# Attention with scaled probabilities turned by plain transposes and neighbourhood outputs written backwards, on one Trainium2 core

## What is computed

```python
s = jnp.einsum('bqhd,bkhd->bhqk', qblk, k).astype(jnp.float32) * scale
p = jax.nn.softmax(s, axis=-1).astype(v.dtype)
return jnp.einsum('bhqk,bkhd->bqhd', p, v)
```

## Time and profile before

| what | value |
|---|---|
| median of 3 runs | 1291.67 us |
| profiled execution | 1291.43 us |
| its span | 1289.6 us |
| mean granted PE clock | 0.934 of 2.4 GHz |
| busy share of the span | PE 88%, PEld 44%, DVE 28%, ACT 22%, POOL 8% |
| DMA | 311.67 MB, 242 GB/s mean |

### The profile page before, as it was taken

How to read it: one execution, slowest core, us unless ns; L and a number is a source line. 1 busy time by engine, 2 the same in 40 slices (tenths; PEclk the granted TensorE clock), 3 DMA queues, 4 the chain that set the end, 5 groups by cost and what they waited for, 6 DMA issues and landing times. The chain is left out here.

```text
span 1289.6 us, 19112 instructions
## 1 busy us (share of the span) xinstructions
PE 1138.2 (88%) x8093; PEld 567.9 (44%) x8093; DVE 366.6 (28%) x884; ACT 277.4 (22%) x673; POOL 103.6 (8%) x111
## 2 busy tenths in 40 slices
PE   4998999984999999999489989999579999999935
PEld 2455466542344444443144545665234444444313
DVE  3102554116122222212140056431512212222214
ACT  1111444113011111111131035430401111111112
POOL 3200000300001101100000010000010101100000
PEclk8999999986999999999679999999779999999975
DMA  9803555343499999998651155531646999999721
GB/s 363 313 16 131 215 196 197 133 175 145 150 368 371 373 373 386 379 376 317 257 188 41 66 197 214 196 131 66 245 151 231 381 366 374 382 387 384 276 107 50
DMA packets 68707, 311.67 MB, mean 242 GB/s; under 512 B 8837, under 2 KB 11105, under 8 KB 46081
## 3 DMA queue, kind: packets, MB, share of 16 engines
q1 hardware_dynamic: 58400, 288.58, 58.6%
q0 software_dynamic: 9344, 18.55, 4.4%
q10 hardware_dynamic: 864, 3.15, 0.6%
HBM read 304.24 MB, written 18.58 MB: 250 GB/s over the span
## 5 line engine op out<-in xcount | busy, mean ns | idle before, releaser
L710 PE MATMUL psum<-arena 128*64 128x512 f32 x512 | 239.0, 611 | 6.3 <-issue 4.9
L713 PE MATMUL psum<-arena 128*64 128x512 f32 x512 | 239.1, 611 | 0.0
L710 PEld LDWEIGHTS psum<-arena 128*64 128x64 f32 x512 | 68.7, 140 | 150.1 <-issue 148.1
L758 PE MATMUL psum<-arena 128*64 128x512 f32 x512 | 126.7, 616 | 2.7 <-ACT arena L1104 2.7
L1428 DVE SCALAR_TENSOR_TENSOR arena<-arena,psum 64x768 f32<-64x768 f32 x32 | 30.3, 948 | 331.2 <-ACT arena L1099 331.2
L721 PE MATMUL psum<-arena 128*32 128x256 f32 x2048 | 117.4, 381 | 0.1
L1099 ACT ACTIVATE arena<-psum 64x768 f32<-64x768 f32 x32 | 25.7, 804 | 314.1 <-PE psum L713 314.1
L721 PEld LDWEIGHTS psum<-arena 128*32 128x32 f32 x2048 | 63.4, 110 | 65.1 <-issue 27.3
L846 PE MATMUL psum<-arena 128*128 128x384 f32 x256 | 83.5, 487 | 1.2 <-PE psum L834 0.6
L987 PE MATMUL psum<-arena 128*128 128x384 f32 x256 | 83.6, 487 | 0.6 <-PE psum L987 0.6
L525 POOL DMA_INDIRECT arena<-token_rows,row_i x32 | 31.0, 970 | 519.4 <-PE psum L693 266.5
(11 more groups left out here) (223 smaller groups left out, 1224.8 us busy)
## 6 DMA issues: line engine op xcount, KB each, us to landing
arena<-in_w_gate SPq DMA_DIRECT2D x64, 1024.0 KB, 10.5
arena<-in_w_up SPq DMA_DIRECT2D x64, 1024.0 KB, 14.9
arena<-in_w_down SPq DMA_DIRECT2D x64, 1024.0 KB, 7.8
arena<-in_w_ada SPq DMA_DIRECT2D x24, 2048.0 KB, 7.8
arena<-in_w_in SPq DMA_DIRECT2D x6, 2048.0 KB, 22.1
arena<-in_w_out SPq DMA_DIRECT2D x4, 2048.0 KB, 7.7
arena<-expert_rows SPq DMA_DIRECT2D x12, 512.0 KB, 8.3
arena<-in_w_in SPq DMA_DIRECT2D x2, 1664.0 KB, 13.1
```

The costliest lines, as they stand in the source:

```text
L710: ins = nc.tensor.matmul(bank[b][0:MAIN, :], hg[:, k, 0:MAIN], wg[half][:, k % 4, :], start=(k == 0), stop=(k == KD - 1))
L713: ins = nc.tensor.matmul(bank[b][MAIN:P, :], hg[:, k, 0:MAIN], wu[half][:, k % 4, :], start=(k == 0), stop=(k == KD - 1))
L758: ins = nc.tensor.matmul(bank[6][MAIN * j:MAIN * j + MAIN, :], hidT[:, c, 0:MAIN], w[half][:, c % 2, 512 * j:512 * j + 512], start=(c == 0 ...
```

## The change

The exponentials are no longer divided by their sums on the way through PE. DVE takes one reciprocal per head as soon as that head's exponentials are there, GpSimd multiplies the head's `prob` (128 by n, in place, in SBUF) by it, and PE turns each block with a plain transpose against the identity, waiting for one head at a time. `exp_ready` is raised once per head. The reversed order of the neighbourhood queries stays in `probT` and in the product with the values; ACT undoes it by writing those outputs backwards. The diagonals and their buffer go. `unit` is moved so that GpSimd's program can use it.

```diff
@@ GpSimd, after the output DMAs of layer l have landed @@
                 pool.sem_inc(out_free, 1)
+                for u in range(UNITS):
+                    n, c = unit(u)[3], 2 * (u % 2)
+                    for i in range(2):
+                        pool.wait_ge(rsum_ready, 2 * (UNITS * l + u) + i + 1)
+                        p = prob[:, u % 2, i, 0:n]
+                        pool.tensor_scalar(p, p, rsum[:, c + i:c + i + 1], None, ALU.mult).then_inc(scaled, 1)
                 if l + 1 < DEPTH:
                     caches(l + 1)
@@ PE, scores @@
-                        pe.wait_ge(exp_ready, UNITS * l + u - 1)
+                        pe.wait_ge(exp_ready, 2 * (UNITS * l + u - 1))
@@ PE, turned @@
-                    pe.wait_ge(diag_ready, UNITS * l + u + 1)
                     for i in range(2):
+                        pe.wait_ge(scaled, 2 * (UNITS * l + u) + i + 1)
                         if u >= 1:
                             pe.wait_ge(probT_act if i == 0 else probT_dve, UNITS * l + u)
                         for c in range(n // P):
-                            ins = nc.tensor.matmul(bank[4 + i][:, P * c:P * c + P], prob[:, u % 2, i, P * c:P * c + P], diag[:, u % 2, i, :],
-                                                   start=True, stop=True)
+                            ins = nc.tensor.transpose(bank[4 + i][:, P * c:P * c + P], prob[:, u % 2, i, P * c:P * c + P], ident)
@@ ACT, exps and outputs @@
-                        ins = nc.scalar.activation(prob[:, u % 2, i, 0:n], bank[c][:, 0:n], ACT.Exp,
-                                                   bias=neg_max[:, c:c + 1],
-                                                   accum_out=sums[:, 2 * (u % 4) + i:2 * (u % 4) + i + 1])
-                    ins.then_inc(exp_ready, 1)
+                        nc.scalar.activation(prob[:, u % 2, i, 0:n], bank[c][:, 0:n], ACT.Exp,
+                                             bias=neg_max[:, c:c + 1],
+                                             accum_out=sums[:, 2 * (u % 4) + i:2 * (u % 4) + i + 1]).then_inc(exp_ready, 1)
...
-                    nc.scalar.activation(hT[:, 4 * kind + pair, P * t:P * t + P], bank[6][:, 0:P], ACT.Copy).then_inc(o_ready, 1)
+                    o = hT[:, 4 * kind + pair, P * t:P * t + P]
+                    if kind == 0:
+                        o = bass.AP(o.tensor, o.offset + P - 1, [list(o.ap[0]), [-1, P]])
+                    nc.scalar.activation(o, bank[6][:, 0:P], ACT.Copy).then_inc(o_ready, 1)
@@ DVE, called in place of diagonals(u) @@
-                def diagonals(u):
-                    kind = unit(u)[0]
+                def reciprocals(u):
                     c, cs = 2 * (u % 2), 2 * (u % 4)
-                    dve.wait_ge(exp_ready, UNITS * l + u + 1)
-                    st.did(v.reciprocal(rsum[:, c:c + 2], sums[:, cs:cs + 2]))
-                    st.sync()
                     for i in range(2):
-                        ins = v.tensor_scalar(diag[:, u % 2, i, :], rev if kind == 0 else ident, rsum[:, c + i:c + i + 1], None, ALU.mult)
-                    ins.then_inc(diag_ready, 1)
+                        dve.wait_ge(exp_ready, 2 * (UNITS * l + u) + i + 1)
+                        v.reciprocal(rsum[:, c + i:c + i + 1], sums[:, cs + i:cs + i + 1]).then_inc(rsum_ready, 1)
```

More of the change, by code:

```diff
@@ L149, in build @@
         qtok = tiles(wide[:, 0:NT * HEADS * QKD], NT)
-        diag = wide[:, 0:512].rearrange("p (u i n) -> p u i n", u=2, i=2)
         extra = take(4 * SMALL)
@@ L199, in build @@
         j_idx = consts[:, C_J:C_J + sum(SPARE)]
-        rev = consts[:, C_REV:C_REV + P]
         quarter = consts[:, C_BLK:C_BLK + 4]
@@ L262, in build @@
         lora_stat, lora_norm, kr_ready, q_roped, kr_spread = (sem(n) for n in ("lora_stat", "lora_norm", "kr_ready", "q_roped", "kr_spread"))
-        bias_added, diag_ready = sem("bias_added"), sem("diag_ready")
+        bias_added, rsum_ready, scaled = sem("bias_added"), sem("rsum_ready"), sem("scaled")
         score_ps, max_ready, exp_ready, probT_ps, probT_act, probT_dve, o_ps, o_ready = (sem(n) for n in (
@@ L356, in overflow, with unit @@
                     eng.sem_inc(s, share)
+        def unit(u):
+            kind, r = divmod(u, 12)
+            pair, t = divmod(r, 3)
+            return kind, pair, t, (P if t == 0 else TOK)
         @block.sync
@@ L609, in copies_qk @@
             copy_out(eng, l, parity, IT_QK, IT_KOUT, place, width=TOK, scale=lambda i: NA_SCALE if i < 4 else 1.0)
[L611 to L614, removed]
         @block.tensor
@@ L1554, in _ @@
                     n = unit(u)[3]
-                    diagonals(u)
+                    reciprocals(u)
                     if u + 2 < UNITS:
```

## The result

The changed kernel takes 1341.9 us (median of 4 runs, 1334.8 to 1352.2) against 1293.6: 1.038 times the time, 95% interval 1.030 to 1.046. It is slower, outside the range of the forecast. The profiled execution took 1347.4 us with a span of 1345.6.

The account below looks back on a forecast made before the run. PE was taken to bound attention, tied to a chain through DVE; the new periods save 49.0-64s us, 13.8 at s=0.55, so 1291.4-13.8 = 1277.6 us. The forecast's own range was 1271 to 1285, the whole range 1267 to 1303.

Parts of the forecast that it names:

- s: Time GpSimd takes to scale one head of 128x384 in the attention loop; taken as 0.55 us.
- four triples of 7.67 + 4s, four of 7.55 + 4s: Attention loop's new periods in us per three units, neighbourhood and latent; before, 10.56 and 10.78.
- the last pass's own time: In DVE's wait to copy B's turned second head: the final transpose pass, put at 0.27 us of 0.58.
- What is s?: Step pricing GpSimd's scaling of 384 elements: 0.45 us by the copy, 0.95 by two-tensor addition, 0.55 taken.
- Rival 4: Clock falls to 1.2 GHz between turning B and C in every triple: 24 us, about 1302; chance 0.03.
- Rival 2: GpSimd becomes the bound, PE waiting in every B and C: at s=0.95, 11.8 us lost, 1303; chance 0.18.
- One pass instead of two: PE's turning in attention: each triple loses 14 passes of 0.118 us, 1.66 us.
- DVE's order: In attention a unit's reciprocal stands behind the previous unit's copy, so raising `exp_ready` per head gains nothing.
- Backward outputs free: ScalarE's reversed output writes in attention cost nothing; its items, half already backwards, lie between 487 and 492 ns.
- GpSimd's queue: Next layer's cache loads stand behind 24 scalings but already waited for the layer's last output, so nothing moves.
- Ceiling of 33.5: Most attention could save, in us, if PE alone set the pace with its stalls gone too.
- Stretches after attention as long as before: What follows attention shifts as a whole, its lengths unchanged.

Follow-up runs that it names:

- e7_fill: The changed kernel with unread products of the identity and ones filling PE's waits for GpSimd; 1321.2 us, ratio 1.021 to the kernel before.
- e12_fill_transposes: The changed kernel with PE's waits for GpSimd filled by useless transposes, in the same passes as products would take; 1318.0 us, ratio 1.019 to the kernel before.
- e6_half: The changed kernel with GpSimd scaling only half of each head's columns, the other half's division left out; 1299.1 us, ratio 1.006 to the kernel before.
- e8_forms: The kernel before with memsets, copy and several forms of product added in GpSimd's idle time in layer 0's attention; 1290.3 us in one run.
- e4_ahead: The changed kernel with VectorE taking reciprocals one unit ahead, scaling still on GpSimd; 1273.7 us, ratio 0.987 to the kernel before.
- e5_backwards: The kernel before with diagonals built from the identity for both kinds and neighbourhood outputs written backwards by ScalarE; 1291.7 us, ratio 1.000.
- e2_no_scale: The changed kernel with the division left out, no reciprocals or scaling, PE waiting for the exponentials only; 1269.3 us, ratio 0.983 to the kernel before.

## Why the prediction was wrong

**The mechanism was right.** The forecast tied the loop to a chain, reciprocal, scaling of two heads, copy, reciprocal, scaling, with four s a triple. With s = 1.22, four triples of 7.67 + 4s, four of 7.55 + 4s and 4.4 us at the ends (89.8 less the eight periods of before) make 104 us a layer. With the clock held, e7_fill and e12_fill_transposes took 104.1. At s = 0.76 e6_half came near the 89 to 90 expected. One term was misread without effect: the last pass's own time, 0.88 less five spacings of 0.118, is 0.29 and not 0.27, 0.3 us over sixteen triples.

**The step that failed is "What is s?"** It bounded s by 0.45, from the copy, and 0.95, from the addition of two tensors, and held the scaling to be near the copy because it has one tensor input. Measured: 1.24 alone and 1.22 from start to start of a pair, beyond the dearer bound. The number of tensors read does not order GpSimd's instructions: in e8_forms the product with a scalar (1.25) is dearer than the product of two tensors (1.00, near the 0.95 that the addition's row gave for two). The bound was not one; it rested on the untested thought that fewer inputs cannot cost more. That step costs 0.67 x 64 = 43 us against s = 0.55, of a miss of 64 (1341.9 against 1277.6): 49 - 64 x 1.22 is 29 us lost, where 14 us gained were forecast. The Trainium skill (GPSIMD Engine Reference, 3.1 Elementwise) gives about 1.8 cycles an element for a tight loop, 512 elements in 769 ns, and calls it the best case; the rows here show 1.24 us for 384, so this operation is dearer than that.

**Rival 4, the clock, came on top,** at a chance of 0.03. Its price came out: 24 us forecast; in the profiled execution attention took 115.0 + 117.6 us against 2 x 104.1 with the clock held, 24.4, and by the medians of runs the fills gave back 20.7 and 23.9. That is in part luck: the forecast had all sixteen triples slow between turning B and turning C, while the clock fell in fourteen and stayed low beyond C's values. The chance was wrong because one stretch ahead of attention was taken for evidence on the loop. The prediction also set the two rivals apart as if one excluded the other. They come together: the longer s, the longer PE's stalls, and with longer stalls the clock was lower (0.96 and 0.92 with half the columns, 0.79 with all, 1.00 once the stalls were filled).

**Rival 2**, at 0.18, had the sign and the place, GpSimd as the bound, with PE waiting for it in B and C. Its price was set at s = 0.95, 12 us lost in place of 29.

**Point by point.** One pass instead of two: right (224 passes fewer). DVE's order makes the earlier `exp_ready` worth nothing: right, and it held the key; e4_ahead changes only that order. Backward outputs free: right (e5_backwards). GpSimd's queue: right, the next layer's cache loads are issued 0.7 us behind the end of attention in both kernels. Ceiling of 33.5: too high, 27 us in attention (e2_no_scale). Stretches after attention as long as before: not quite, 1.5 and 2.5 us longer.

## What to carry to other kernels

Before work moves to another engine, find where its input becomes ready and where that engine's predecessor issues it: with the same GpSimd instruction the kernel lost 48 us when the reciprocals stood in one place of VectorE's order, some 21 to 24 of it by the clock, and gained 17 when they stood one unit earlier. Where no row prices an operation, a row of a different operation is no bound, however much more that one seems to do; leave the far end open and let the chain's multiplier, here 64 us for each us, say how wide. And where a change makes PE wait again and again in short pieces, count the clock's loss together with the wait, not as a separate accident.

## What the runs showed of the hardware

GpSimd's product of 128x384 float32 with one scalar per partition took 1.24 to 1.25 us, with a constant 1.16, with the scalar spread as a second tensor 0.83, with a second full tensor 1.00; a copy 0.50. VectorE did the product with the scalar in 0.42. TensorE's clock fell to 1.2 GHz in every neighbourhood triple of the changed kernel, each time after two stalls close together, of 1.57 to 2.22 and 0.59 to 0.67 us. Filling the stalls with useless transposes or products held it at 1.00 in attention and made the kernel 21 to 24 us faster. Why a product with a scalar is dearer on GpSimd than one with a tensor stays open.
